# Leaving out the unread identity products of TensorE in a two-layer decoder trunk

## The reference

```python
hn = rmsnorm(h, norm_mix[0]);  h += retention(hn, w_in, gn, w_out)    # 4 heads, one chunk of 256
hn = rmsnorm(h, norm_ffn[0]);  h += (silu(hn @ w_gate) * (hn @ w_up)) @ w_down       # d_ff 3584
hn = rmsnorm(h, norm_mix[1]);  h += s5(hn, ...)     # diagonal complex state space, 64 groups, then a GLU
hn = rmsnorm(h, norm_ffn[1]);  h += moe(hn, router, w_gate, w_up, w_down)   # 8 experts, top 2 a token
return rmsnorm(h, norm_final)
```

## Time and profile before

| | us |
|---|---|
| three runs | 1580.07, 1582.07, 1582.33; median 1582.07 |
| the profiled execution, its own time | 1582.01 |
| its span | 1580.2 |

### The profile page before, as it was taken

One profiled execution on the slowest core, in us unless ns is written; L12 is line 12 of the kernel. 1 busy time (PEld: TensorE's weight loads), 2 busy tenths in 40 slices (PEclk: granted clock), 3 DMA queues, 4 the chain that ended last, 5 costly groups with the idle time before them and its releaser, 6 DMA issues.

```text
span 1580.2 us, 23620 instructions
## 1 busy us (share of the span) xinstructions
PE 1565.6 (99%) x9486; PEld 1306.9 (83%) x9486; DVE 1211.2 (77%) x825; ACT 981.9 (62%) x732; POOL 271.4 (17%) x244
## 2 busy tenths in 40 slices
PE   9999999999999999999999999999999999999997
PEld 8788889999988888888888888888888888888886
DVE  5556566555557758888888888888888888888897
ACT  5443444333454357777777777777777777777775
POOL 5599315300037108100000000000000000000100
PEclk9999999999999999999999999999999999999999
DMA  9644647855511368999999999999999999999993
GB/s 350 173 159 154 207 147 286 282 200 186 186 54 57 115 247 317 394 391 365 386 363 365 384 367 362 386 365 363 382 373 350 379 376 356 388 374 356 397 393 143
DMA packets 202143, 469.18 MB, mean 297 GB/s; under 512 B 7784, under 2 KB 20288, under 8 KB 202064
## 3 DMA queue, kind: packets, MB, share of 16 engines
q1 hardware_dynamic: 199872, 461.13, 80.7%
q0 software_dynamic: 2048, 6.88, 1.4%
q10 hardware_dynamic: 144, 0.07, 0.0%
HBM read 461.23 MB, written 15.21 MB: 302 GB/s over the span
## 4 chain that ended last, share of the span: by engine, by line
PE 94%; DVE 2%; ACT 2%; POOL 1%; issue 1%; DMA 0%; ACTq 0%; DVEq 0%; POOLq 0%
PE PS L1744 90%; PE PS L1862 2%; DVE weights_lo L1263 1%; ACT weights_hi L884 1%; POOL b_padded L784 1%; PE PS L2075 0%; ACT c_padded L884 0%; PE PS L2234 0%; DVE residual L1263 0%; POOL param_tmp L643 0%; DMA constants<-in_constants 0%; PE PS L1832 0%; ACT x_transposed_hi L934 0%; DVE act_rows L1263 0%; POOL param_tmp L640 0%
## 5 line engine op out<-in xcount | busy, mean ns | idle before, releaser
L1263 DVE TENSOR_TENSOR weights_lo<-weights_raw,weights_hi 128x2048 fp32r<-128x2048 f32 (+1 forms) x419 | 962.0, 2305 | 256.6 <-ACT weights_hi L884 255.0
L884 ACT ACTIVATE weights_hi<-weights_raw 128x2048 fp32r<-128x2048 f32 (+1 forms) x419 | 800.8, 1912 | 364.7 <-PE PS L1744 353.4
L1744 PE MATMUL PS<-weights_hi,gathered_hi 128*128 128x512 f32 x896 | 355.2, 396 | 0.3 <-DVE gathered_lo L1625 0.3
L1744 PE MATMUL PS<-weights_hi,gathered_lo 128*128 128x512 f32 x896 | 355.2, 396 | 0.0
L1744 PE MATMUL PS<-weights_lo,gathered_hi 128*128 128x512 f32 x896 | 352.2, 393 | 0.0
L1744 PE MATMUL PS<-weights_hi,act_transposed_hi 128*128 128x512 f32 x624 | 253.0, 405 | 0.3 <-DVE act_transposed_lo L1422 0.3
L1744 PE MATMUL PS<-weights_hi,act_transposed_lo 128*128 128x512 f32 x624 | 247.0, 396 | 0.0
L1744 PE MATMUL PS<-weights_lo,act_transposed_hi 128*128 128x512 f32 x624 | 245.7, 394 | 0.0
L1744 PEld LDWEIGHTS PS<-weights_hi,gathered_lo 128*128 128x128 f32 x896 | 168.2, 188 | 41.3
L1744 PEld LDWEIGHTS PS<-weights_lo,gathered_hi 128*128 128x128 f32 x896 | 168.2, 188 | 41.2
L1744 PEld LDWEIGHTS PS<-weights_hi,gathered_hi 128*128 128x128 f32 x896 | 168.2, 188 | 39.9 <-DVE gathered_lo L1625 0.4
(11 more groups left out here) (283 smaller groups left out, 1273.3 us busy)
## 6 DMA issues: line engine op xcount, KB each, us to landing
weights_raw<-in_moe_w_up SPq DMA_DIRECT2D x111, 1024.0 KB, 7.2
weights_raw<-in_moe_w_down SPq DMA_DIRECT2D x111, 1024.0 KB, 6.9
weights_raw<-in_moe_w_gate SPq DMA_DIRECT2D x110, 1024.0 KB, 7.1
weights_raw<-in_ret_w_in SPq DMA_DIRECT2D x24, 1024.0 KB, 6.7
weights_raw<-in_ffn_w_gate SPq DMA_DIRECT2D x14, 1024.0 KB, 5.1
weights_raw<-in_ffn_w_up SPq DMA_DIRECT2D x14, 1024.0 KB, 5.1
weights_raw<-in_ffn_w_down SPq DMA_DIRECT2D x14, 1024.0 KB, 4.9
weights_raw<-in_ret_w_out SPq DMA_DIRECT2D x8, 1024.0 KB, 4.9
```

The lines of the kernel that those rows point to most:

```text
L884: return nc.scalar.activation(o, i, ACT.Copy)
L1263: return nc.vector.tensor_tensor(o, a, b, op)
L1744: return nc.tensor.matmul(o, l, r, start=start, stop=stop)
```

## The change

`idle_work` and all its eleven calls are left out. All waits stay where they were; the six opening products and every other instruction stay too.

```diff
--- before.py
+++ after.py
@@ -1960,11 +1960,6 @@
                     down(STEPS - 1, 1, FFN_UNITS - 1)
 
 
-            def idle_work(n, bank):
-
-                for _ in range(n):
-                    mm(PS[:, bank, 0:P], ident, ident, True, True)
-
             pe.wait_ge(warm_ready, 1)
             for _ in range(6):
                 mm(PS[:, 5, 0:P], act_rows[:, 0, SEQ:SEQ + P], act_rows[:, 0, SEQ:SEQ + P], True, True)
@@ -1973,13 +1968,9 @@
             pe.wait_ge(g_landed, 64)
             nc.tensor.transpose(PS[:, 7, 0:7 * KT], gain_rows[0:7 * KT, :],
                                 cst[0:7 * KT, C_IDENT:C_IDENT + 7 * KT]).then_inc(gains_t, 1)
-            idle_work(4, 5)
             pe.wait_ge(xhi_ready, 1)
-            idle_work(3, 5)
             pe.wait_ge(xhi_ready, 2)
-            idle_work(3, 5)
             pe.wait_ge(first_hi_half, 1)
-            idle_work(3, 5)
 
             def first_unit():
 
@@ -2056,14 +2047,12 @@
                                                   cst[0:PAIRS, C_IDENT:C_IDENT + PAIRS])
                     ins.then_inc(par_t, 1)
             turn_y(HEADS - 1)
-            idle_work(10, 0)
             head_out(HEADS - 1, 0, RET_UNITS - 2)
             pe.wait_ge(yt_lo, 2 * HEADS)
             closing_unit(RET_UNITS - 1, ht_hi[0], ht_lo[0])
 
 
             plain(1)
-            idle_work(9, 4)
             dense()
 
 
@@ -2165,8 +2154,6 @@
                 if q:
                     pe.wait_ge(bt_copied, 2 * q + 1)
                     turn_b(q, 1, 6)
-                else:
-                    idle_work(3, 5)
                 s5_in(q)
                 if q:
                     s5_out(q - 1)
@@ -2192,7 +2179,6 @@
                     ins = nc.tensor.transpose(PS[:, 2 * t + kt // 4, kt % 4 * P:(kt % 4 + 1) * P],
                                               resid[:, t, kt * P:(kt + 1) * P], ident)
                 ins.then_inc(hnt_done, 1)
-                idle_work((4, 0)[t], 4)
             pe.wait_ge(router_ready, 1)
             for t in range(TT):
                 pe.wait_ge(hnt_copied[t], 1)
@@ -2203,16 +2189,12 @@
                         tokens = slice(32 * i, 32 * i + 32)
                         ins = mm(PS[tokens, 6, t * EXPERTS:(t + 1) * EXPERTS], hn_t[:, t, kt, tokens], router[:, kt, :],
                                  kt == 0, kt == KT - 1)
-                if t == 0:
-                    idle_work(2, 4)
             ins.then_inc(logits_done, 1)
-            idle_work(9, 4)
             pe.wait_ge(chosen_done, 1)
 
             mm(PS[:, 6, 32:32 + EXPERTS], tri, chosen[:, 0, :], True, True)
             mm(PS[:, 6, 40:40 + EXPERTS], ones, chosen[:, 0, :], True, False)
             mm(PS[:, 6, 40:40 + EXPERTS], tri, chosen[:, 1, :], False, True).then_inc(rank_done, 1)
-            idle_work(4, 4)
 
 
             def turned(kt):
```

## The result

Without the 54 products the kernel takes 1591.81 us (median of 4 runs, 1591.11 to 1592.97); before, 1582.05. The ratio is 1.0063 (95% interval 1.0051 to 1.0075). The forecast was 1586.2 and its range ended at 1590.3: right in direction, less than half of the size.

The account below looks back on a forecast made before the run. TensorE was taken as the bound after its first real product. Start +2.15, three places 0, router -0.3 and +2.5 sum to +4.35 on 1582.01, 1586.4, given as 1586.2 us; 8-in-10 range 1581.9 to 1590.3.

Parts of the forecast that it names:

- After the last head, and after the second transposes: Removing 10 and 9 products opens holes of 2.6 and 2.3 us; cost 0 each, upper bound 2.8 each.
- Only TensorE's stream differs: Whole kernel: other engines and DMAs keep their streams, no wait is added; stages outside the named stretches stay as long.
- Start, +2.15: 13 products before the first real product: without them 5 us at half pace, part swallowed, net +2.15 us.
- Router, +2.5 for the clock and -0.3 for the products in the way: 19 router products: low clock from the gather on costs +2.5 us; products no longer delaying the chain give -0.3.
- S5's three products, 0: S5 stage: TensorE would wait for POOL's work on b_padded anyway, so removing the three products gains 0.
- Half pace at the lower level: TensorE's clock is 1.2 GHz instead of 2.4, so half of the time spent there is lost.
- Rival A: Only the start costs; small products and router records keep the clock up at 592: 1583.9 us, chance 0.28.
- the second rule: Skill page: uninterrupted long waits make TensorE cold, not short ones with products between; router costs nothing, start remains.
- Rival B: Transposes count for nothing, so holes at last head and dense layer lengthen, up to 2.8 each: 1590 us, chance 0.17.
- C: The clock stays up everywhere, every clock price is nothing and -0.3 is left: 1581.7 us, chance 0.09.
- D: Products do not cover the clock, only cost issue time: at most 12.1 us back; ruled out, no chance given.

Follow-up runs that it names:

- no_head_dense: The kernel before without the 10 products after the last head and the 9 after the second transposes, the other products kept: 1586.15 us, ratio 1.0024.
- tiny: The kernel before with all 54 products kept but shrunk from 128x128 to 32 rows of output by 8 columns: 1588.98 us, ratio 1.0046.
- half: The kernel before with 5 of 10 products after the last head, 4 of 9 before the dense layer, 4 of 9 and 2 of 4 at the router: 1584.21 us.
- wide: The kernel before with equally long cover after the last head and second transposes, from fewer products, some of 512 columns: 1583.66 us, ratio 1.0012.
- no_start: The kernel before without the 13 identity products at the start, the other 41 kept: 1585.30 us, ratio 1.0022.
- no_router: The kernel before without the 19 products around the router: 1583.95 us, ratio 1.0011.
- no_s5: The kernel before without the three products in the first quarter of the S5 stage: 1581.93 us, ratio 1.0001.
- turns: The kernel before with each identity product replaced by two transposes of the identity: 1580.46 us, ratio 0.9990.
- turns_rest: The kernel before with two transposes for each product everywhere but at the 9 ahead of the dense layer: 1581.74 us, ratio 1.0001.

## Why the prediction was wrong

Its own steps, in order:

- *After the last head, and after the second transposes: "Both are shorter than 4.2 ... I take 0 for each."* This is the step that failed. Holes of 2.6 and 2.2 us did lower the clock, at +1.55 and +1.52. The only fall that the trace of before had, after 4.8 us, shows that such a hole is enough, not that a shorter one isn't; I used it as a threshold. Both profiles with holes of 2.2 to 2.6 us at these places, after and `no_head_dense`, had the fall (one of the ten executions of `no_head_dense` has a mean granted clock of 0.998 and may lack one). So had `tiny`, with waits of 1.8 and 1.5 us behind small products; the profile of `half`, with 1.5 and 1.3 behind full ones, had not, though others of its executions probably did.
- *"Only TensorE's stream differs ... Nothing is moved past a queue and no wait is added."* The term that this left out, at nothing, was missing too. The products were also instructions, and with them gone every later one lies elsewhere in the blocks in which TensorE's stream is fetched: 2.2 us in S5. `wide` and `tiny` show it from both sides, with the clock up and with it down. The prediction had said that every other stage should be as long as before; this one was not.
- *Start, +2.15*: +1.88 from the first real product on, and +1.32 against before's, because that product came 0.56 earlier, by chance. Low for 5.03 us, where I took 5; swallowed at 30.57, where I said 0.35, 0.35 in this trace (1.77 to 1.42). In `no_start` 1.58 is left.
- *Router, +2.5 for the clock and -0.3 for the products in the way*: +2.39 and -0.12, and the gather does start at the lower level. The clock fell in every profile in which the products lacked or did no work, but three executions of `no_router` leave room for the doubt.
- *S5's three products, 0*: right, `no_s5`.
- *Half pace at the lower level*: right, 23 records against 45.
- *Rival A* fell with the router, and with it the second rule that the prediction took from the page of the Trainium skill: the longest wait there was 2.4 us, with small products before and behind, and the clock fell. *Rival B* had four falls, but for a reason that `turns` refutes; its 1590 comes nearest by chance (its own price, 2.8 a place, would make up to 1591.8 and not 1591.2). *C* fell at once. *D* fell as argued.

With 0 replaced by 3.1 for the two holes and 2.2 added for the fetch, the sum would have been 4.35 + 3.1 + 2.2 = +9.65, beside a measured +9.8. That these meet is in part luck: start and router cost 3.6 in the trace where the sum has 4.35, and 1.1 us of the trace is the late transfer at the end.

## What to carry to other kernels

Where TensorE is the bound, filling its waits with work that nobody reads is no waste: here 12 us of it in the waits saves some 7 us of half pace behind them. Transposes of the identity did as well. A single observed fall gives an upper bound for the hole that is harmless, never a lower one, so price each hole from zero to half the low stretch and let the range say so. One profile shows one execution: where the others have another granted clock, the same hole went otherwise in them. And an instruction that is removed moves all behind it: look for idle pieces of the engine that the profile puts down to issue, above all in stretches of small matmuls.

## What the runs showed that I had not expected

- The clock reached its upper level on constant products and input transposes alone. After, TensorE had issued nothing else when it stopped at 7.9 us, and the column falls from 1.00 to 0.72 in the slice 10 to 11, which it can only do from above. When it rises differs: at 5.2 us in `turns_rest`, with three of the 16 transposes started, and only at 10.5, among the identity products, in `no_s5`.
- The fall can come after the work has begun again: after, TensorE restarted at 208.10 and the level fell at 208.42. The stretch is then lost in full. Where a hole lies in it, as the wait for `pick` at the router, part of it is free.
- Small products (32 rows by 8 columns) in the waits did not hold the clock in `tiny`; the 108 transposes of `turns`, one for each record of the products, did.
- The instruction fetch can stop TensorE for 1.0 to 1.9 us at a time, and with next to no data in the way: the DMA share is 0.00 around the stop of `wide`.
